# Two layers of a hybrid backbone: the first token groups of layer 1's input projection, one channel block at a time in place of two side by side

## The reference

```python
h = rmsnorm(x, norm_pre) * (1 + scale) + shift
z = jnp.einsum('bld,de->ble', h, w_in)                    # 1024 -> 2832 columns
u_pool, g_pool, q, k, v, g_attn, qkv_d, b_d, a_d, g_delta = jnp.split(z, points, axis=-1)
...                                                       # mixers on the parts
y = jnp.einsum('ble,ed->bld', gates * branches, w_out)
x = x + gate * rmsnorm(y, norm_post)
```

## Time and profile before

| | |
|---|---|
| median of 3 runs | 1732.21 us (1730.95 to 1732.43) |
| the profiled execution | 1731.49 us |
| its span, first to last instruction | 1729.7 us |
| TensorE busy (matmuls) | 1637.1 us, 95% |
| TensorE weight loads busy | 1343.1 us, 78% |
| VectorE, ScalarE, GpSimd busy | 1001.0, 621.3, 924.0 us |

### The profile page before, as it was taken

One profiled execution on the slowest core, in us unless ns is written; L12 is line 12 of the kernel. 1 busy time (PEld: TensorE's weight loads), 2 busy tenths in 40 slices (PEclk: granted clock), 3 DMA queues, 4 the chain that ended last, 5 costly groups with the idle time before them and its releaser, 6 DMA issues. The chain is left out here.

```text
span 1729.7 us, 40122 instructions
## 1 busy us (share of the span) xinstructions
PE 1637.1 (95%) x17250; PEld 1343.1 (78%) x17250; DVE 1001.0 (58%) x1471; ACT 621.3 (36%) x1260; POOL 924.0 (53%) x854
## 2 busy tenths in 40 slices
PE   4899999989998999999999999998999899999998
PEld 2788999978997655556879999997899765555586
DVE  2664243827774777779238513382777477777911
ACT  4411231124444444455234123112444444445511
POOL 1000389029992587885320047911999358788532
PEclk9899999999999999999999999999999899999999
DMA  9345312210000000113321211231000000010422
GB/s 340 137 159 172 105 32 89 80 62 16 16 4 12 14 13 27 34 36 136 123 89 38 64 39 51 62 102 60 22 17 4 12 14 13 20 40 21 152 95 77
DMA packets 69776, 112.37 MB, mean 65 GB/s; under 512 B 9824, under 2 KB 41824, under 8 KB 69600
## 3 DMA queue, kind: packets, MB, share of 16 engines
q1 hardware_dynamic: 69136, 109.62, 18.8%
q10 hardware_dynamic: 464, 0.17, 0.0%
HBM read 90.30 MB, written 19.47 MB: 63 GB/s over the span
## 5 line engine op out<-in xcount | busy, mean ns | idle before, releaser
L1670 POOL TENSOR_TENSOR attn_accp<-attn_accp,attn_pr 128x1024 f32<-128x1024 f32 x110 | 269.4, 2449 | 42.9 <-ACT attn_pr L1736 37.2
L94 PE MATMUL ps<-in_h_hi,in_w_hi 128*128 128x384 f32 x720 | 244.1, 339 | 2.5 <-DVE in_h_lo L615 2.5
L96 PE MATMUL ps<-in_h_hi,in_w_lo 128*128 128x384 f32 x720 | 242.4, 337 | 0.0
L1940 DVE TENSOR_REDUCE attn_ql<-ps 128x1 f32<-128x1152 f32 x128 | 172.5, 1355 | 102.3 <-PE ps L1858 102.0
L1736 ACT ACTIVATE attn_pr<-ps 128x512 f32<-128x512 f32 x292 | 158.7, 595 | 170.7 <-PE ps L1902 161.8
L1901 PEld LDWEIGHTS ps<-attn_QH,attn_KH 128*128 128x128 f32 x292 | 55.5, 190 | 122.1 <-ACT attn_pr L1736 55.2
L94 PEld LDWEIGHTS ps<-in_h_hi,in_w_hi 128*128 128x128 f32 x720 | 135.7, 188 | 9.3 <-issue 7.5
L1911 PE MATMUL ps<-attn_pr,z 128*64 128x512 f32 x520 | 139.5, 615 | 0.0
L1144 POOL TENSOR_TENSOR delta_ML<-delta_EK,local 128x256 f32<-128x256 f32 x180 | 130.4, 746 | 15.2 <-PE ps L1184 14.5
L96 PEld LDWEIGHTS ps<-in_h_hi,in_w_lo 128*128 128x128 f32 x720 | 135.5, 188 | 0.0
L1901 PE MATMUL ps<-attn_QH,attn_KH 128*128 128x512 f32 x292 | 131.5, 450 | 0.0
(11 more groups left out here) (308 smaller groups left out, 3857.0 us busy)
## 6 DMA issues: line engine op xcount, KB each, us to landing
in_w<-in_w_in SPq DMA_DIRECT2D x21, 1024.0 KB, 5.1
z<-in_w_mod SPq DMA_DIRECT2D x8, 2048.0 KB, 8.0
gates<-in_gate SPq DMA_DIRECT2D x48, 192.0 KB, 1.9
attn_gt<-gates SPq DMA_DIRECT2D x34, 256.0 KB, 2.6
z<-in_x_sample SPq DMA_DIRECT2D x16, 512.0 KB, 6.0
zz<-in_w_mod SPq DMA_DIRECT2D x4, 2048.0 KB, 13.4
out_w<-in_w_out SPq DMA_DIRECT2D x16, 512.0 KB, 5.7
out_y<-z SPq DMA_DIRECT2D x16, 512.0 KB, 2.9
```

The costliest lines, as they stand in the source:

```text
L94: nc.tensor.matmul(out, a_hi(i), b_hi(i), start=(i == 0), stop=False)
L96: last = nc.tensor.matmul(out, a_lo(i), b_hi(i), start=False, stop=(i == n - 1))
L1670: nc.gpsimd.tensor_tensor(acc, a, pr[:, n % 4], ALU.add).then_inc(pool_added, 1)
L1940: nc.vector.tensor_reduce(ql[:, a % 4, blk, HD:HD + 1], ps[:, bank:bank + 3, 0:GRP], AX_XY, ALU.max).then_inc(mx_read, 1)
```

## The change

In `side_by_side` the two loops are exchanged: `a` is the outer loop and `k` the inner one. The waits for `h_done` are kept on the first pass only (`a == 0`). The turn of tile 7 or 8, which stood behind `k == 1` (12 matmuls), stands behind `(a, k) == (0, 3)` (12 matmuls). The matmuls, their operands and their banks are the same.

```diff
-            for k in range(KD):
-                pe.wait_ge(h_done, KD * g + k + 1)
-                for a in range(2):
+            for a in range(2):
+                for k in range(KD):
+                    if a == 0:
+                        pe.wait_ge(h_done, KD * g + k + 1)
                     out, ch = ps[:, ring(2 * g + a), 0:GRP], slice(P * a, P * a + P)
                     nc.tensor.matmul(out, hi[:, k, ch], h_hi[:, k, tk], start=(k == 0), stop=False)
                     nc.tensor.matmul(out, hi[:, k, ch], h_low(k, tk), start=False, stop=False)
                     last = nc.tensor.matmul(out, lo[:, k, ch], h_hi[:, k, tk], start=False, stop=(k == KD - 1))
                     if k == KD - 1:
                         last.then_inc(product, 1)
-                if g < 2 and k == 1:
-                    x_turn(pe, NT - 2 + g)
+                    if g < 2 and (a, k) == (0, 3):
+                        x_turn(pe, NT - 2 + g)
```

## The result

The changed kernel takes 1735.26 us (median of 19 runs, 1730.03 to 1739.84) against 1729.55 us (19 runs, 1724.22 to 1732.43) of the kernel before on the same chips: ratio 1.0037, interval 1.0028 to 1.0047. It is slower, by 6.4 us as the ratio says and 5.7 as the medians do.

The account below looks back on a forecast made before the run. TensorE, busy 95% of the span, was taken to bound the kernel. Delays of 2.95 us at group 1 and 4.27 at group 2 reached 4.85 at the next chunk: 1736.34 on the profiled execution, forecast 1736.9, full range 1734.8 to 1738.6.

Parts of the forecast that it names:

- TensorE sets the stage from 905.39 on: Layer 1's input projection: a microsecond TensorE loses in the edited function should arrive whole at the stage's end.
- the absorbing rival: Behind 932.8, the stage's pace doesn't move with TensorE: up to 0.4 us given back, in the limit all; chance 0.05.
- Arrivals release half the work; +4.85: Edited function: each low part's arrival releases three matmuls instead of six; next chunk starts 4.85 us late.
- the bound of 5.3: Upper end of the summed loss in the edited function: 0.1 us more at each of the stops.
- The turn is moved past two more arrivals, and the square of tile 8 waits for it: Group 0: turn needs four arrivals instead of two, ending 1.2 us later; ScalarE's square starts 0.32 later.
- Group by group: 2.95, then 1.9 more: Group 1 begins 2.95 us late, group 2 4.27 late, the next chunk 4.85 late.
- The rival in which only group 0 counts: Groups 1 and 2 run without a stop; loss stays at 2.95 us, time 1735.1; chance 0.09.
- The clock stays up: Edited function: granted clock stays 1.00; rival, a fall at the new stops, 1737 to 1742 us, chance 0.05.
- The price of up to 5.0: Clock-fall rival: dense work at the lower clock loses up to 5.0 us on top of the 4.85.
- The next chunk at 937.6: Behind group 2: next chunk's first matmul at 937.6, today 932.77; a start before 936.5 would make the forecast wrong.
- The range of 1734.8 to 1738.6: Full range of the whole kernel's time, reaching down to the first rival and up into the short clock fall.
- Gain zero from an earlier first bank: Each group's first block completes earlier, but first eviction moves from 929.17 to about 932.1 and nothing waits; gain zero.

Follow-up runs that it names:

- the undisturbed run: Changed kernel plus 12 idle matmuls in the old stop ahead of group 0, new stops empty; 32.44 us from group 0 to next chunk, ratio 1.0027.
- the turns-early run: Changed kernel with turns behind (a, k) = (0, 1) in place of (0, 3), stops unfilled; ratio to the kernel before 1.0029 (1.0015 to 1.0043).
- the two with fillers: Changed kernel plus idle matmuls: 38 in old and new stops, ratio 1.0032; or 12 ahead of group 0 alone, ratio 1.0027.

## Why the prediction held, point by point

- **TensorE sets the stage from 905.39 on.** Right. The projection behind the border takes 265.09 us against 265.08, so the absorbing rival is out: the whole loss of the border stays.
- **Arrivals release half the work; +4.85.** Right. At full clock the loss is 5.06. From group 0's start the undisturbed run has its stops' ends at 2.83, 4.73, 6.83, 17.99 and 26.91; my sum had 2.78, 4.66, 6.70, 17.85 and 26.78. The border itself is 32.44 against 32.23. The missing 0.2 is 0.05 at the first stop, 0.13 by the third, nothing more at the next two, and 0.08 behind the last; the bound of 5.3 had 0.1 for each stop. And 0.08 of the 0.2 isn't the order's, since group 0 starts that much sooner behind the fillers.
- **The turn is moved past two more arrivals, and the square of tile 8 waits for it.** Right, seen in the releaser of the square. I put 0.32 on that directly; undisturbed, the square starts 4.61 us behind group 0's start in place of 4.15, 0.46 later. The turns' place as a whole is worth 1.41, since the copy of tile 8 feeds group 2.
- **Group by group: 2.95, then 1.9 more.** Measured alone: 3.08 and 1.99. The rival in which only group 0 counts is out.
- **The clock stays up.** Wrong. A granted clock under 1 between 903 and 940 was one of the forecast's own signs of being wrong, and it came. I held the stop of 1.9 us ahead of group 0 harmless, since one execution had kept 1.00 behind it, and gave a fall 0.05. All three profiles of the changed kernel had one. Against 32.44, the falls cost 2.11, 0.41 and 2.85 us, 1.8 on average. The price of up to 5.0 was for dense work; 10.1 us of low clock cost 2.85, since much of a fall lies on waits. A section of the Trainium skill (TensorE: Matmul & The Clock Gate, "A second HAM failure mode: psum-queue depth-cycling") tells of another kernel, in which short idles between groups of matmuls, frequent enough, make the clock swing. These profiles agree only in part: the turns-early run fell at 912.3 behind new stops of 1.10 and 0.94 us, but the run with only the old stop filled had new ones of 0.97, 0.22, 1.31 and 1.07 and kept 1.00.
- **The next chunk at 937.6.** It came at 936.19, before the 936.5 that I had named as a sign of being wrong, but only since that execution reached group 0 3.75 us earlier. Counted from group 0's start it is 34.55 us, with the two falls, against the forecast's 32.23.
- **The size.** In part luck. The range of 1734.8 to 1738.6 held 1735.26 because the kernel before was itself measured 2.7 us lower in these runs than in the three that I had, while the difference was larger than my 4.85; the ratio of 1.0037 on my base of 1732.21 gives 1738.6, the very end of the range. 5.06 and 1.8 make 6.9 us. The three ratios of the changed kernel say 6.4 (4.8 to 8.1), 4.2 and 6.7 us, and the two with fillers, whose profiles had no fall, 5.5 and 4.7. So the timed runs bear out the order's 5 us and can't tell whether the falls add to it.
- **Gain zero from an earlier first bank.** Right: the evictions start behind the last high part, at 930.59 in the changed kernel's first execution, and nothing waits for them.

```profile
930.59 1.96 ACT L939 ACTIVATE zz<-ps 128x384 f32<-128x384 f32 x5
```

**Open:** what the first falls have to do with the change. They began 0.8, 0.4 and 1.4 us behind group 0's start, ahead of any new stop. At 0.4 us only the first three matmuls had started, and they are the same in both orders; so what comes later in the function can't have caused that one. Yet the four profiles with group 0 in the changed order and no fillers all had a fall in the border (the turns-early one at 6.4 us, behind two new stops), the four with group 0 side by side and the same stop of 1.9 us ahead of it had none (three of the kernel before and the one with only groups 1 and 2 changed), and the four with fillers ahead of group 0 had none. Four against four may be chance, and it isn't shown that the kernel before never falls here. The 5.06 us don't hang on it, as they are a difference of profiles at full clock; the 1.8 do.

## What to carry to other kernels

Where a product is fed block by block by a slower chain, let each arrival release as much work as it can: what counts at the end is the work left behind the last arrival, here 27 matmuls of 0.176 us in place of 3, less the slack that TensorE's backlog gives: for groups 1 and 2 alone the 24 more are 4.2 us of work and cost 1.99. When a reorder moves a step past waits, look for who waits for that step on other engines; the turns, which were not the point of the edit, made 1.4 of the 5.06 us. And price a clock fall beside any place that already has a stop of 2 us: one profile without it shows little.

## What the runs showed of the hardware that was not expected

- The granted clock fell behind a stop of 1.9 us in three executions (0.8, 0.4 and 1.4 us after work had begun again), and in five others with the same stop it held through as many microseconds. The first of the three had two low pieces of some 3.3 us with as much at full clock between them, the second one of 3.3, the third one of 10.1.
- One such short piece cost 0.41 us where matmuls waited for arrivals right behind it, and 1.45 where they were dense.
- Idle matmuls of 256 columns in a stop cost nothing measurable: 12 ahead of group 0, where it then started 2.20 us behind the last matmul before the stop in place of 2.28, and 26 in the later stops, with a border of 32.43 against 32.44 without these. The clock stayed at 1.00 in both runs.
